# A hybrid decoder step on one core: GpSimd's operations on 1024 columns written as four on 256 columns

## The reference

```python
def swiglu(h, wg, wu, wd):
    return (jax.nn.silu(h @ wg) * (h @ wu)) @ wd

def ssd_recurrent(xdt, a, bm, cm, s0):
    def step(S, inp):
        xt, at, bt, ct = inp
        S = S * jnp.exp(at)[..., None, None] + jnp.einsum('bgrp,bgn->bgrpn', xt, bt)
        return S, jnp.einsum('bgrpn,bgn->bgrp', S, ct)
    ...

def trunk(x, pos0, ret_s, gdn_s, gdn_buf, ssm_s, ssm_buf, chunked):
    for i in range(DEPTH):
        h = rmsnorm(x, norm_mix_w[i])
        ...
        x = x + out.astype(x.dtype)
        x = x + swiglu(rmsnorm(x, norm_ffn_w[i]), ffn_w_gate[i], ffn_w_up[i], ffn_w_down[i]).astype(x.dtype)
    y = rmsnorm(x, norm_final_w)
```

## Time and profile before

| | |
|---|---|
| median of 3 runs | 3354.7 us (3343.66 to 3355.53) |
| profiled execution | 3348.94 us, span of its instructions 3347.0 us |
| busy: PE, PEld | 3146.6 us (94%), 3030.8 us (91%) |
| busy: DVE, ACT, POOL | 1755.0 us (52%), 797.0 us (24%), 1010.3 us (30%) |
| POOL: CAST, subtraction | 230 of 1115 ns, 230 of 2619 ns on average |
| POOL: L520, L524, L527, L529 | 16 each, of 1898, 1958, 2732 and 2933 ns on average |

### The profile page before, as it was taken

The page is one execution under the profiler, slowest core; times in us unless marked ns, Lnnn a source line. Parts: engine busy times, 40 slices in busy tenths (PEclk is TensorE's granted clock), DMA queues, the critical chain, the costliest instruction groups (busy, mean ns, idle before and its releaser), DMA issues.

```text
span 3347.0 us, 46815 instructions
## 1 busy us (share of the span) xinstructions
PE 3146.6 (94%) x20090; PEld 3030.8 (91%) x20090; DVE 1755.0 (52%) x2023; ACT 797.0 (24%) x1174; POOL 1010.3 (30%) x528
## 2 busy tenths in 40 slices
PE   6999899998799999999988999999969999999997
PEld 5899888888799999999977898989958999999997
DVE  5344657556643333333477868778586333333335
ACT  4222414314320000000145414243253100000002
POOL 2222201101023333333233536345352333333331
PEclk9999999999899999999999999999999999999999
DMA  4121101101011111111113214132230111111111
GB/s 145 59 71 58 49 26 33 39 26 39 20 44 46 50 45 51 45 45 51 38 48 103 95 58 146 63 107 83 84 124 26 55 45 50 45 47 49 45 51 64
DMA packets 94474, 198.15 MB, mean 59 GB/s; under 512 B 21796, under 2 KB 52164, under 8 KB 94152
## 3 DMA queue, kind: packets, MB, share of 16 engines
q1 hardware_dynamic: 52384, 150.03, 13.4%
q10 hardware_dynamic: 41896, 45.23, 4.4%
HBM read 171.41 MB, written 19.59 MB: 57 GB/s over the span
## 4 chain that ended last, share of the span: by engine, by line
PE 75%; DVE 14%; ACT 5%; issue 3%; DMA 2%; POOL 1%; ACTq 1%; SPq 0%; DVEq 0%; POOLq 0%
PE ps_set L566 63%; PE ps_core L837 4%; ACT work L1114 3%; PE ps_set L575 3%; DVE work L1932 1%; ACT L1114 1%; DVE work L2041 1%; DVE work L1691 1%; DVE work L2302 1%; DVE h_lo L1702 1%; DVE work L2282 1%; DVE work L2321 1%; DMA work<-ssm_cum_rows 1%; DMA x<-in_x 1%; PE ps_set L661 0%
## 5 line engine op out<-in xcount | busy, mean ns | idle before, releaser
L492 POOL CAST w_hi<-w_raw 128x1024 fp32r<-128x1024 f32 x230 | 256.5, 1115 | 2176.4 <-PE ps_set L566 1969.1
L566 PE MATMUL ps_set<-h_hi,w_hi 128*128 128x344 f32 x3648 | 803.9, 329 | 14.9 <-ACT work L1114 13.5
L566 PE MATMUL ps_set<-h_lo,w_hi 128*128 128x344 f32 x3648 | 774.5, 321 | 0.0
L566 PE MATMUL ps_set<-h_hi,w_lo 128*128 128x344 f32 x3648 | 771.6, 320 | 0.0
L566 PEld LDWEIGHTS ps_set<-h_hi,w_hi 128*128 128x128 f32 x3648 | 614.4, 189 | 39.9 <-issue 19.0
L566 PEld LDWEIGHTS ps_set<-h_lo,w_hi 128*128 128x128 f32 x3648 | 617.4, 189 | 0.0
L566 PEld LDWEIGHTS ps_set<-h_hi,w_lo 128*128 128x128 f32 x3648 | 609.5, 188 | 0.0
L495 POOL TENSOR_TENSOR w_lo<-w_raw,w_hi 128x1024 fp32r<-128x1024 f32 x230 | 602.3, 2619 | 18.4
L1797 DVE TENSOR_TENSOR x<-x,ps_set 128x1032 f32<-128x1032 f32 x160 | 196.7, 1229 | 255.6 <-PE ps_set L566 255.6
L1114 ACT ACTIVATE work<-work 128x1032 f32<-128x1032 f32 (+5 forms) x190 | 179.4, 958 | 524.5 <-DVE work L2150 447.8
L566 PE MATMUL ps_set<-y_hi,w_hi 128*128 128x344 f32 x1296 | 282.1, 326 | 5.7 <-ACT work L1114 5.7
(11 more groups left out here) (229 smaller groups left out, 3618.9 us busy)
## 6 DMA issues: line engine op xcount, KB each, us to landing
w_raw<-in_w SPq DMA_DIRECT2D x230, 512.0 KB, 3.3
work<-ssm_cum_rows ACTq DMA_DIRECT2D x32, 512.0 KB, 4.1
sample<-in_ssm_state SPq DMA_DIRECT2D x16, 512.0 KB, 4.3
out_ssm_s<-sample SPq DMA_DIRECT2D x16, 512.0 KB, 2.6
x<-in_x SPq DMA_DIRECT2D x6, 688.0 KB, 14.8
work<-work ACTq DMA_DIRECT2D x16, 258.0 KB, 2.4
out_y<-x SPq DMA_DIRECT2D x6, 688.0 KB, 3.4
sample<-bc_rows SPq DMA_DIRECT2D x8, 512.0 KB, 5.3
```

The lines of the kernel that those rows point to most:

```text
L492: return nc.gpsimd.tensor_copy(w_hi[:, k, :], w_raw[:, k, :])
L566: mm = nc.tensor.matmul(out[:, g, 0:TN], w[:, slot, cols], v[:, g * TN:(g + 1) * TN], start=(start and n == 0), stop=(stop and n == 2))
```

## The change

The functions `high` and `low` in GpSimd's program, which work on the 1024 columns of a weight unit, go over four parts of 256 columns; a new function `state_op` does the same with the four operations on a decode state, two requests (2 x 128 columns) at a time. Each returns its last instruction, so that the semaphore that was raised by the one operation is raised by the last of four. No wait, no buffer, no transfer and nothing on another engine is changed.

```diff
+        QUARTERS = [slice(j * 256, (j + 1) * 256) for j in range(4)]
...
             def high(k):
-                return nc.gpsimd.tensor_copy(w_hi[:, k, :], w_raw[:, k, :])
+                for part in QUARTERS:
+                    ins = nc.gpsimd.tensor_copy(w_hi[:, k, part], w_raw[:, k, part])
+                return ins
 
             def low(k):
-                return nc.gpsimd.tensor_tensor(w_lo[:, k, :], w_raw[:, k, :], w_hi[:, k, :].bitcast(F32), ALU.subtract)
+                for part in QUARTERS:
+                    ins = nc.gpsimd.tensor_tensor(w_lo[:, k, part], w_raw[:, k, part], w_hi[:, k, part].bitcast(F32), ALU.subtract)
+                return ins
+
+            def state_op(out, in0, in1, op):
+                for b in range(0, ND_TOK, 2):
+                    ins = nc.gpsimd.tensor_tensor(out[:, b:b + 2], in0[:, b:b + 2], in1[:, b:b + 2], op)
+                return ins
...
-                    nc.gpsimd.tensor_tensor(UPDATE, B_ROWS, spread(XD8[:, 8 * t:8 * t + 8], P), ALU.mult)\
+                    state_op(UPDATE, B_ROWS, spread(XD8[:, 8 * t:8 * t + 8], P), ALU.mult)\
                         .then_inc(*ssm_pool.step(n(f"xB{t}")))
...
-                    nc.gpsimd.tensor_tensor(S_TILE, S_TILE, spread(work[:, 12, col:col + 8], P), ALU.mult)\
+                    state_op(S_TILE, S_TILE, spread(work[:, 12, col:col + 8], P), ALU.mult)\
                         .then_inc(*ssm_pool.step(n(f"Sx{t}")))
                     pool.wait_ge(*ssm_pool.value(n(f"Sx{t}")))
-                    nc.gpsimd.tensor_tensor(S_TILE, S_TILE, UPDATE, ALU.add).then_inc(*ssm_pool.step(n(f"Sn{t}")))
+                    state_op(S_TILE, S_TILE, UPDATE, ALU.add).then_inc(*ssm_pool.step(n(f"Sn{t}")))
                     pool.wait_ge(*ssm_pool.value(n(f"Sn{t}")))
-                    nc.gpsimd.tensor_tensor(UPDATE, S_TILE, C_ROWS, ALU.mult).then_inc(*ssm_pool.step(n(f"SC{t}")))
+                    state_op(UPDATE, S_TILE, C_ROWS, ALU.mult).then_inc(*ssm_pool.step(n(f"SC{t}")))
```

## The result

| | before | after |
|---|---|---|
| median | 3354.7 us | 3374.7 us |
| profiled execution | 3348.94 us, span 3347.0 | 3374.15 us, span 3372.1 |
| busy: DVE, POOL | 1755.0, 1010.3 us | 1636.3, 1406.6 us |
| ratio to before | | 1.0074 [1.006, 1.0088] |

The change costs 0.74% [0.60, 0.88], some 25 us. The forecast was 3362 us, 13 us above the profiled execution of before; the time lies inside the range given with it, the sign is the one forecast, the size is twice that.

What follows compares the result with a forecast made beforehand. TensorE was busy 94% of the span, with GpSimd's decode chain itself a bound in the state-space groups. Terms 1 + 12 + 6 - 6 = +13 us on 3348.9 gave 3362 us, range 3296 to 3398.

Steps and rivals of the forecast that it cites:

- The decode chain: GpSimd's state operations and weight splits in each state-space group: 3.0 us longer per group, +12 us in four groups.
- 48 instructions more: From a group's first late L520 to its end, 16 operations become four instructions each: 48 x 0.10 = 4.8 us.
- turns with VectorE: VectorE operations on two SBUF operands get in between GpSimd's quarters in the group's cycles and tail: 2.7 us per group.
- idle time used up: GpSimd's idle 2 x 1.76 us before L520 in a group is used up first, taking 3.5 us off.
- head start: VectorE, blocked only for a quarter, reaches a group's first sum some 1.0 us earlier, taken off the group's cost.
- I take two thirds: The turns in a group's cycles and tail (+1.8, +1.8, +0.5) were called an upper count and taken as 2.7.
- The dense run behind the decode state: VectorE's some 25 us from L2307 on: cutting brings no relief, +1.9 us in each of three groups, +6 us.
- every VectorE operation lets one quarter in: In the dense run after the decode state, each VectorE operation admits one GpSimd quarter until all eight are through.
- The lone places and the unit pairs: Lone blocked VectorE operations, as L2168, wait for one quarter only: -6 us; splits where two units end together: +1 us.
- Relief: Rival, chance 0.22: blocked VectorE operations wait for a quarter only, 0.69 us at most; kernel faster by 55, 3294 us.
- No hand-over between quarters: Rival, chance 0.10: the queued next quarter keeps the ports, VectorE is blocked as long as now; 3358 us.
- The fixed cost sets the group's end: Rival, chance 0.23: above 0.11 us per quarter, each decode chain's 48 instructions outrun its idle time; 3408 us at 0.26.

## Why the prediction was right or wrong

**What bounds the kernel.** Right for the change, half right for the kernel before. Cutting the state operations alone costs most of what the change costs, and after it GpSimd waits for no later sum. But in the kernel before the chain is the last to end only at a group's last sum, where VectorE waits 14.1 us in all; at the sums ahead of it GpSimd waits for VectorE, 1.76 us at each of the later two. With some 4 us for each load taken out of GpSimd's chain the time fell by 10 us, not by 18 or more, because VectorE was close behind.

**The decode chain: the term that was mis-sized.** It said 4.8 + 2.7 - 3.5 - 1.0 = 3.0 us a group, +12 in all; measured were 5.8, 5.9, 7.4 and 7.2, 26.2 in all. By its own parts, in the first group (the others were not taken apart):

| | forecast | measured |
|---|---|---|
| 48 instructions more | 4.8 (0.10 each) | 6.6 (0.138 each) |
| turns with VectorE | 2.7 | 4.2 |
| state's load lands later or sooner | - | -0.6 |
| idle time used up | -3.5 | -3.5 |
| head start | -1.0 | -0.9 |
| sum | 3.0 | 5.8 |

The line on turns is what is left of the time once the others are taken, with their errors in it; that turns cost time can be read in place: `xB` grew from 1.90 to 3.21 us though four parts that nothing blocks take 0.43 more, as `Sx` does (2.33 against 1.90 in other cycles). The first failed step is the fixed cost, taken from a memset on one column (0.10 us); the operations themselves pay 0.13 to 0.14. The second is "I take two thirds" of the count of turns: as far as a remainder can tell it came in full, 4.2 against the 4.1 counted. Both went the same way, and since 4.5 of the 7.5 us are taken off before anything remains, errors of 1.8 and 1.5 us doubled the result. The price from which the text said the fixed cost decides, 0.11 us, fits: the measured one lies above it, and the kernel is slower.

By the Trainium skill (GPSIMD Engine Reference, section 3.1) the forecast had an estimate of 0.18 us for it, and 3385 us; the runs show 0.13 to 0.14 and 3374.7, between that and the forecast.

**The dense run behind the decode state: wrong sign.** Forecast +1.9 in three groups. In the first the last sum started at 1882.20 and at 1889.09 after. The run ends where TensorE takes up the next projection, on the chain of waits of before and of after:

```profile
1912.31 9.71 PE ps_set L566 x60
```

```profile
1918.14 13.95 PE ps_set L577 x87
```

That is 30.11 against 29.05 us, -1.06; in the others it was -1.0. Little of it lasts: up to the next group's first `xB` 0.2, 0.1 and 0.6 us are left. The step that failed is "every VectorE operation lets one quarter in", priced with the whole 0.69 or 0.36 us of a quarter. The turns are as forecast, one for each operation, but a turn costs less. VectorE in front of the first group, before:

```profile
1794.55 2.37 DVE L1935 COPY conv_s<-work 128x8 f32<-128x8 f32 x1
1796.84 1.27 DVE L1932 SCALAR_TENSOR_TENSOR work<-work,ssmc 128x1024 f32<-128x1024 f32 x1
1798.04 0.18 DVE L1938 TENSOR_TENSOR taps<-conv_s,ssmc 128x32 f32<-128x32 f32 x1
1798.15 1.28 DVE L1932 SCALAR_TENSOR_TENSOR work<-work,ssmc 128x1024 f32<-128x1024 f32 x1
```

and after, against the four quarters of one subtraction:

```profile
1795.11 0.70 DVE L1946 COPY conv_s<-work 128x8 f32<-128x8 f32 x1
1795.72 1.84 DVE L1943 SCALAR_TENSOR_TENSOR work<-work,ssmc 128x1024 f32<-128x1024 f32 x1
1797.48 0.72 DVE L1949 TENSOR_TENSOR taps<-conv_s,ssmc 128x32 f32<-128x32 f32 x1
1798.12 1.81 DVE L1943 SCALAR_TENSOR_TENSOR work<-work,ssmc 128x1024 f32<-128x1024 f32 x1
```

Before, one operation pays 2.37 - 0.16 = 2.2 us and three pay nothing. After, the four pay 0.54, 0.57, 0.54 and 0.53: 2.2 again. A quarter of a subtraction takes 0.69 us on GpSimd and costs VectorE 0.54; a quarter of a CAST, 0.36, costs some 0.2 (in the dense run of the first group an operation of 1.22 us takes 1.42 beside one). Four and four of them cost 3.0 us, what the whole split cost before, where the forecast had 4.2. By its own terms, in the first group: L2307 took 2.62 us for all four and takes 2.28, -0.3 and not +0.7; from L2315 up to L1931 it was 17.02 and is 16.97 us, even and not +1.2; from there to the end of the convolution 7.70 and 7.03, -0.7 where even was forecast. Where the two small gains come from was not separated.

**The lone places and the unit pairs.** Forecast -6 and +1. The kernel with quarters outside the groups alone measures both together: +1 us [-2, +4], not -5. The blocked time did go (L2168 from 2711 to 971 ns at most), but TensorE gained nothing by it. The chain of waits at the end of the first feed-forward part, before:

```profile
1650.01 3.63 DVE y_lo L2168 x2
...
1654.57 11.65 PE ps_set L575 x72
```

and after:

```profile
1650.15 2.10 POOL w_hi L495 x4
...
1652.33 2.81 POOL w_lo L500 x4
...
1655.18 9.92 PE ps_set L586 x61
```

Before, TensorE stood from 1649.48 to 1654.57, 5.09 us, with the blocked L2168 on the path. After, it stands from 1650.03 to 1655.18, 5.15 us, for the split: cut in four it lets VectorE in, ends later, and TensorE waits for its last part. Near the end of the kernel the same place has 5.10 and 5.14 us. So the -4.2 that the forecast counted for the two came to +0.1; the step that failed is that it followed only the operation that is freed and took the split there to be waited for by nobody. At the first pair TensorE starts at 62.69 instead of 61.94, +0.75, against the 0.55 of the forecast. The 0.15 us that it took off as slack is there still, 0.14 from the split's last part to TensorE (62.55 to 62.69). The first `xB` of the first group starts between 1808.8 and 1814.8 us in the five kernels with quarters ahead of it, and between 1804.9 and 1810.5 in the four without, so no gain is left there. The remaining terms were not separated.

**Luck.** Outside the chains the forecast had +1 - 6 in the lone places and pairs and +6 in the dense runs, +1 in all; the span has -1.1. The terms of -6 and +6 were wrong by some 6 us each, in opposite directions, so that the total is off by 12 us, where the decode chain alone is off by 14.

**The rivals.** Relief fell on the place where it was to decide: the cycles do not gain. Its view of the lock was half right. The Trainium skill (SBUF — State Buffer, Who interferes with whom) has the shared ports held for the whole instruction, and a shorter one does hold them for less: L2302 is blocked for at most 0.55 us now (1232 ns against 682). But the next quarter comes in behind every VectorE operation, and time that VectorE wins in a cycle is worth nothing while GpSimd sets the pace. "No hand-over between quarters" is out: all four operations above are blocked, for a quarter each. "The fixed cost sets the group's end" came in part: at 0.14, not at 0.26, it gives 1.8 us a group more than forecast, and the turns 1.5.

**The signs to look for.** Four quarters of the CAST take 1.43 us, 0.36 each; L2302 lasts 1.23 us at most, the later waits of GpSimd in front of L520 are gone, the wait for the decode state rose, the first group ends at 1918.14 instead of 1912.31, and the feed-forward parts keep their length (from the first L2168 to the last 681.9 us before and 681.5 after, in either part): all as written.

## What to carry to other kernels

Cutting an engine's operations so that another gets in sooner moves time between the two, so ask first which of them sets the pace of the stage: here GpSimd had 1.76 us of room in a cycle of 19.58, and 18 more instructions at 0.14 us used it up. Take the fixed cost of an instruction from operations of its own kind at two widths, not from a memset, and where an estimate is a small difference of large terms, carry each term's error to the end. Where an operation is cut so that another is freed, look for what waits for its last part: at the end of the feed-forward parts that was TensorE. A drop in an engine's busy time is no gain by itself: 119 us less on VectorE went with 25 us more in all.

## What the runs showed of the hardware that was not expected

- The price of one more GpSimd instruction, back to back, is 0.13 us for a CAST and 0.14 for an operation on two inputs, the same with parts of 512, 256 and 128 columns.
- GpSimd and VectorE take strict turns: with GpSimd's next quarter already queued, one quarter gets in behind each VectorE operation that takes part, and a quarter of a subtraction costs the next operation 0.53 to 0.57 us, though the quarters alone stand 0.69 apart. With eight parts they stand 0.42 apart (60.30 to 61.98 for four) and one costs L1868 0.25 (1.48 us against 1.23 at its shortest). That the missing 0.14 to 0.17 us are the fixed cost, in which VectorE is not held up, fits both widths and was not tried by itself.
- Eight parts lose more at a unit pair (4.8 us) than their added instructions explain: 14 x 0.14 = 2.0. The rest is turns with VectorE's operations, of which each lets only one short part through.
